# Two groups of value projections: the seven products in another order, and the last product's weight low parts made by a DMA

## Chip, core and metric

The kernel runs on one core of one Trainium2 chip. The metric is the device time of the whole program in microseconds, as the median of several executions.

## What is computed

Two transformer-like blocks over 512 tokens of 1,024 features. The change lies in the last mixer, hgrn2. Cut to what matters:

```python
def hgrn2_mixer(h, w_in, lb, norm_g, w_out):
    u = h @ w_in                              # (512, 1024) @ (1024, 8192)
    q, fz, i, gate = jnp.split(u, 4, axis=-1)
    ...                                       # i holds the values of 16 heads, 128 columns each
    o = hgrn2_chunk_scan(qc, kc, vc, bc)
    ...
    return (o * jax.nn.silu(gate)) @ w_out
```

The change touches only how `i`, the values (512 tokens by 2,048 columns), is projected.

## The kernel before

**Arithmetic.** Every fp32 operand of a matmul is kept as a high part, the fp32 value copied to the fp32r type that TensorE reads, and a low part, the value minus the high part. A product is three matmuls: high by high, high by low, low by high. ScalarE makes the high parts of the weights (an ACTIVATE that copies `RAW` to `WH`), VectorE the low parts (a TENSOR_TENSOR, `WL` = `RAW` - `WH`).

**The value stage.** The 2,048 value columns are done in two groups (`v` = 0 and 1 in `VG`). In each group the operands are cut in two by two blocks and seven products of block sums take the place of eight (Strassen's scheme in Winograd's form). The seven products carry the numbers 1 to 7: 1, 2 and 3 read a weight block as it came from memory (`b11`, `b21`, `b22`), 4 to 7 read a block into which VectorE has added or subtracted others in `block_sum`. Products 7, 6, 5 and 3 also need summed hidden states, made once and used by both groups: ScalarE makes their high parts (`ZR`, line 2716) and VectorE their low parts (`ER`, line 1784, four instructions for a product).

**Turns.** Each product comes in two halves (`u` = 0, 1), each with one 128 x 1024 weight tile and twelve 128x512 matmuls. This text calls a half a *turn*: `BLOCKS` lists 28 of them, turn 0 to turn 27, fourteen for a group, in the order of `BLOCK_ORDER`. Four buffers (`NS` = 4) hold weights for turns, so a turn uses the buffer of the turn four before it: ScalarE can write turn m's high part once TensorE has done with turn m - 4, and three turns lie between that moment and TensorE's need.

**Order of work.** Nothing is scheduled by a tool: each engine's program is written out by hand and runs in that order. On VectorE, `block_low(m)` makes the low part of turn m and behind some turns issues block sums for later ones, `hidden_low` makes a product's four `ER` parts, and `block_taken` adds a finished product's banks to the result (line 2026). On ScalarE, `block_high(m)` makes the high part (line 2866), `block_copied` copies a finished product out of two PSUM banks (line 2875) and so frees them, and `forget(0)`, `query(0)`, `scan_gate(0)` and `forget(1)` are gate work for the first two heads of the scan, put between. A product may start only when the banks it writes are free (`claim`). Banks 0 and 1 serve products 1, 6, 5 and 3 of the first group in turn.

**Loads.** SyncE issues all weight loads, 512 KB each, in one order (`load`, line 567). A load waits until the VectorE instruction that last needs its buffer is done. The tiles are kept in `RAW` and in parts of `TMP` and `Z` that are idle then. GpSimd has no program of its own.

TensorE's lines 1046, 1048 and 1049 are the three matmuls of a step in this stage. Lines 649 to 651 are those of the ordinary projections, and the first of them after the stage ends it.

Of the kernel before, what the change touches and what calls it, by code (L numbers as in the profile page):

```python
# [57 lines left out]
V1 = V0 + 8 * len(VG)  # L58
BLOCK_ORDER = (1, 7, 6, 2, 5, 4, 3)
BLOCKS = [(p, v, u) for v in range(len(VG)) for p in BLOCK_ORDER for u in range(2)]  # L60
# [83 lines left out]
def raw_list():  # L144
# [3 lines left out]
    for i, (name, n, _) in enumerate(UNITS):  # L148
        if NR <= i < NR + NX:
            slot = i  # L150
        elif name == "ada" and n >= 40:
            slot = NR + NX + n % 2
        elif name == "hgrn_in" and V0 <= n < V1:
            v, quarter, u = (n - V0) // 8, (n - V0) % 8 // 2, n % 2
            if v == 0 and quarter in (0, 3):
                slot = ring % NR
                ring += 1
                held[quarter, u] = slot
            else:
                slot = ((held[0, u], NR + NX + 4 + u, held[3, u], NR + NX + 2 + u) if v else  # L160
                        (None, NR + NX + 2 + u, NR + NX + 4 + u))[quarter]
        else:
            slot = ring % NR
            ring += 1
# [124 lines left out]
def build(nc, a):  # L289
    with ExitStack() as ctx:  # L290
# [133 lines left out]
        def block_source(m):  # L424
            p, v, u = BLOCKS[m]
            return raw(block_unit({1: 0, 6: 0, 3: 1, 7: 2, 5: 2, 2: 3, 4: 3}[p], v, u))

# [3 lines left out]
        def block_bank(p, v):  # L431
            return {7: 2, 4: 2, 2: 4}.get(p, 6 * v)

# [108 lines left out]
        hidden_done = Count(sem("s_hidden"))  # L542
        normed = Count(sem("s_normed"))
        wfree, zfree = {}, {}

# [8 lines left out]


        def sync_program(e):
            def load(i):
# [5 lines left out]
                elif RSLOT[i] >= NR + NX + 2 and RBEFORE[i] is None:  # L563
                    e.wait_ge(square.sem, square.of("pout", "x", 3))
                elif RBEFORE[i] is not None:
                    e.wait_ge(taken.sem, taken.of(RBEFORE[i]))
# [41 lines left out]
        def tensor_program(e):  # L608
# [422 lines left out]
            def block_product(p, v):  # L1031
# [268 lines left out]
        def vector_program(e):  # L1300
# [681 lines left out]
            def block_sum(p, v, u):  # L1982

                b11, b22, b12, b21 = (raw(block_unit(q, v, u)) for q in range(4))
                if p == 7:
                    e.wait_ge(*landed(block_unit(1, v, u)))
                    e.wait_ge(*landed(block_unit(2, v, u)))
                    to, x, y, op = b12, b22, b12, ALU.subtract
                elif p == 6:
# [13 lines left out]
            def block_low(m):  # L2003
                if m >= len(BLOCKS):
                    lo_to(p.unit + m - len(BLOCKS) + 1)
                    return
                i, v, u = BLOCKS[m]
                e.wait_ge(copied.sem, copied.of("block", m))
                hi, lo = block_place(m)
                e.tensor_tensor(lo, block_source(m), hi.bitcast(F32), ALU.subtract).then_inc(  # L2010
                    taken.sem, taken("block", m))
                for q in {5: (0, 2), 4: (3,), 3: (1,)}.get(i, ()):
# [98 lines left out]
            def first_sums():  # L2111
                hidden_sums("pout")
                block_low(0)
                hidden_low("pout", 7)
                block_low(1)
                hidden_low("pout", 6)
# [244 lines left out]
        def scalar_program(e):  # L2361
# [494 lines left out]
            def block_high(m):  # L2856
# [4 lines left out]
                if i in (1, 2, 3):  # L2861
                    e.wait_ge(*landed(block_unit({1: 0, 2: 3, 3: 1}[i], v, u)))
# [48 lines left out]
            def first_sums():  # L2911
                block_high(0)
                hidden_sum("pout", 7)
                block_high(1)
                for i in (6, 5, 3):
                    hidden_sum("pout", i)
# [180 lines left out]


        for program in (tensor_program, vector_program, scalar_program):
            program(Nothing())  # L3100
# [15 lines left out]
        def _(e):  # L3116
            vector_program(e)

        @block.scalar
# [120 lines left out]
```

## Time and profile before

| | before |
|---|---|
| median of 3 runs | 1406.69 us (1406.57 to 1407.81) |
| the profiled execution, its time | 1407.22 us |
| the profiled execution, its span | 1405.4 us |
| TensorE busy | 1390.7 us, 99% |
| VectorE busy | 983.0 us, 70% |
| ScalarE busy | 648.6 us, 46% |
| GpSimd busy | 0.2 us |
| mean busy share of the DMA engines by the window 0 to 100 us | 0.70 |
| the same, 900 to 1000 us | 0.30 |

The span runs from the first to the last instruction of the profiled execution, its time has 1.8 us more around it. An engine's busy time is the sum of its instructions with overlaps counted once. A high busy share of TensorE does not say how near it is to its peak, since matmuls overlap in its pipeline.

### The profile page before, as it was taken

The page shows a single profiled execution, that of the slowest core. Times are in us where ns is not written, and L with a number is a line of the kernel's source. Part 1 is how long each engine was busy: PE and PEld are TensorE (multiplying, and loading weights), DVE is VectorE, ACT ScalarE, POOL GpSimd, SP SyncE. Part 2 cuts the span into 40 slices and gives each one's busy share as a digit, 9 for nine tenths or more (in the row PEclk, how much of TensorE's full clock was granted, in tenths as well). Part 3 has the DMA queues.
Part 4 walks back from the last instruction along what each step waited for, and adds up shares of the span by engine and source line. Part 5 has one row for each costly group of instructions (what it writes and reads, how often), then busy time and mean ns, then how long its engine had stood idle before and what let it go on. Part 6 is the DMA issues. An engine that isn't in the chain of part 4 may idle for free.

```text
span 1405.4 us, 22088 instructions
## 1 busy us (share of the span) xinstructions
PE 1390.7 (99%) x8666; PEld 1190.9 (85%) x8666; DVE 983.0 (70%) x1922; ACT 648.6 (46%) x1268; POOL 0.2 (0%) x4
## 2 busy tenths in 40 slices
PE   8999999999999999999999999999999999999998
PEld 7888888999998888888888888978888888888886
DVE  7887777799953335755466535599798889888645
ACT  6423355567662324542332323575345555556441
POOL 0000000000000000000000000000000000000000
PEclk9999999999999999999999999999999999999999
DMA  9656441254333234032332233213322222221221
GB/s 353 226 186 243 150 162 68 91 172 146 117 107 105 90 103 152 31 105 90 103 107 75 91 116 124 91 47 121 104 91 75 76 76 77 75 76 61 76 75 60
DMA packets 43734, 158.00 MB, mean 112 GB/s; under 512 B 4848, under 2 KB 5232, under 8 KB 43632
## 3 DMA queue, kind: packets, MB, share of 16 engines
q1 hardware_dynamic: 43344, 156.39, 32.5%
q8 instruction: 69, 1.13, 0.3%
q14 instruction: 33, 0.27, 0.1%
q10 hardware_dynamic: 288, 0.21, 0.0%
HBM read 154.48 MB, written 2.10 MB: 111 GB/s over the span
## 4 chain that ended last, share of the span: by engine, by line
PE 95%; DVE 2%; issue 1%; ACT 1%; DMA 0%; SPq 0%; DVEq 0%; ACTq 0%
PE PS L649 26%; PE PS L651 25%; PE PS L650 25%; PE PS L990 3%; PE PS L992 3%; PE PS L991 3%; PE PS L1046 2%; PE PS L1048 2%; PE PS L1049 2%; PE PS L1147 1%; PE PS L1151 1%; PE PS L1139 1%; PE PS L645 1%; PE PS L1079 1%; PE PS L1160 0%
## 5 line engine op out<-in xcount | busy, mean ns | idle before, releaser
L649 PE MATMUL PS<-HH,WH 128*128 128x512 f32 (+1 forms) x880 | 337.3, 383 | 0.0
L651 PE MATMUL PS<-HH,WL 128*128 128x512 f32 (+1 forms) x880 | 332.8, 378 | 0.0
L650 PE MATMUL PS<-HL,WH 128*128 128x512 f32 (+1 forms) x880 | 332.5, 378 | 0.0
L2376 ACT ACTIVATE WH<-RAW 128x1024 fp32r<-128x1024 f32 x176 | 185.3, 1056 | 132.3 <-PE PS L651 86.7
L1371 DVE TENSOR_TENSOR WL<-RAW,WH 128x1024 fp32r<-128x1024 f32 x176 | 213.8, 1219 | 19.0 <-ACT WH L2376 18.6
L651 PEld LDWEIGHTS PS<-HH,WL 128*128 128x128 f32 x880 | 165.5, 188 | 31.3
L649 PEld LDWEIGHTS PS<-HH,WH 128*128 128x128 f32 x880 | 165.6, 188 | 30.7
L650 PEld LDWEIGHTS PS<-HL,WH 128*128 128x128 f32 x880 | 165.7, 188 | 29.3
L649 PE MATMUL PS<-WH,ZH 128*128 128x512 f32 x400 | 155.9, 390 | 0.0
L651 PE MATMUL PS<-WH,ZL 128*128 128x512 f32 x400 | 155.6, 389 | 0.0
L650 PE MATMUL PS<-WL,ZH 128*128 128x512 f32 x400 | 155.6, 389 | 0.0
L1422 DVE TENSOR_TENSOR ZL<-Z,ZH 128x512 fp32r<-128x512 f32 x52 | 35.6, 691 | 136.7 <-ACT ZH L2441 136.7
L2441 ACT ACTIVATE ZH<-Z 128x512 fp32r<-128x512 f32 x52 | 32.4, 632 | 149.2 <-PE PS L651 149.2
L651 PEld LDWEIGHTS PS<-WH,ZL 128*128 128x128 f32 x400 | 75.1, 188 | 15.7
L649 PEld LDWEIGHTS PS<-WH,ZH 128*128 128x128 f32 x400 | 75.1, 188 | 15.5 <-ACT Z L2751 0.2
L650 PEld LDWEIGHTS PS<-WL,ZH 128*128 128x128 f32 x400 | 75.1, 188 | 15.5
L990 PE MATMUL PS<-HH,WH 128*128 128x256 f32 x192 | 54.5, 284 | 1.4 <-DVE Z L1838 1.4
L992 PE MATMUL PS<-HH,WL 128*128 128x256 f32 x192 | 54.3, 283 | 0.0
L991 PE MATMUL PS<-ER,WH 128*128 128x256 f32 x192 | 54.3, 283 | 0.0
L2062 DVE RECIPROCAL DG<-W 128x96 f32<-128x96 f32 (+1 forms) x64 | 48.8, 814 | 0.0
L649 PE MATMUL PS<-WH,HH 128*128 128x512 f32 x96 | 39.2, 408 | 2.0 <-DVE RAW L1331 2.0
L2468 ACT ACTIVATE TMP<-X 128x1024 f32<-128x1024 f32 x18 | 19.0, 1056 | 47.9 <-DVE X L1486 29.9
(348 smaller groups left out, 2625.4 us busy)
## 6 DMA issues: line engine op xcount, KB each, us to landing
RAW<-in_w_fc SPq DMA_DIRECT2D x64, 512.0 KB, 3.3
RAW<-in_hgrn_in SPq DMA_DIRECT2D x56, 512.0 KB, 3.3
RAW<-in_pool_in SPq DMA_DIRECT2D x40, 512.0 KB, 3.3
RAW<-in_ada SPq DMA_DIRECT2D x36, 512.0 KB, 4.5
RAW<-in_w_in SPq DMA_DIRECT2D x26, 512.0 KB, 5.2
RAW<-in_pool_out SPq DMA_DIRECT2D x16, 512.0 KB, 3.3
RAW<-in_hgrn_out SPq DMA_DIRECT2D x16, 512.0 KB, 3.3
Z<-in_ada SPq DMA_DIRECT2D x12, 512.0 KB, 4.4
```

The source lines that it names most:

```text
L649: e.matmul(out, wh, xh, start=first, stop=False)
L650: e.matmul(out, wh, xl, start=False, stop=False)
L651: return e.matmul(out, wl, xh, start=False, stop=last)
L990: e.matmul(out, wh[:, k, :], xh[k], start=fresh and k == 0, stop=False, skip_group_check=True)
L991: e.matmul(out, wh[:, k, :], xl[k], start=False, stop=False, skip_group_check=True)
L992: mm = e.matmul(out, wl[:, k, :], xh[k], start=False, stop=k == 3, skip_group_check=True)
L1046: e.matmul(out, xh[k][:, cols], wh, start=k == 0 and p in (1, 2, 7), stop=False, skip_group_check=True)
L1371: e.tensor_tensor(lo, raw(i), hi.bitcast(F32), ALU.subtract).then_inc(taken.sem, taken(i))
L1422: e.tensor_tensor(lo, Z[:, k, :], hi.bitcast(F32), ALU.subtract).then_inc(zlo.sem, zlo(z))
L2062: e.reciprocal(i8[:, n, l], w8[:, n, l]).then_inc(own.sem, own("iw", h, i))
L2376: e.activation(place(s)[0], raw(i), ACT.Copy).then_inc(whi.sem, whi(s))
L2441: e.activation(z_place(z)[0], Z[:, k, :], ACT.Copy).then_inc(zhi.sem, zhi(z))
```

## The change

It does three things. (1) `BLOCK_ORDER` becomes 1, 2, 6, 7, 5, 4, 3, so that the two products that need no block sum (1 and 2) come first. The weight tiles are laid out in memory and loaded in the order `b11`, `b21`, `b22`, `b12`, the sums move to other turns, and products 2, 7 and 4 change banks. (2) The hidden parts of products 6 and 7 swap places, those of 5 and 3 move some turns later on VectorE, and two MEMSETs move from the stage's start to behind turn 9. (3) For product 3 (turns 12, 13, 26 and 27) VectorE no longer makes the low part. ScalarE writes the negated high part into `WL` by a second ACTIVATE behind the first, and GpSimd then issues a DMA that reads the weight tile from memory again and adds it to `WL`. TensorE waits for that DMA, and SyncE's loads into those tiles' buffers wait for ScalarE's second ACTIVATE.

```diff
-BLOCK_ORDER = (1, 7, 6, 2, 5, 4, 3)
+BLOCK_ORDER = (1, 2, 6, 7, 5, 4, 3)
...
         def block_bank(p, v):
-            return {7: 2, 4: 2, 2: 4}.get(p, 6 * v)
+            return {7: 4, 4: 4, 2: 2}.get(p, 6 * v)
...
+        ADDED = [m for m in range(len(BLOCKS)) if BLOCKS[m][0] == 3]
+        def block_added(m):
+            return s_added[block_slot(m)], 16 * sum(block_slot(x) == block_slot(m) for x in ADDED if x <= m)
...
+        last_blocks = {block_unit(2, v, u): m for m, (p, v, u) in enumerate(BLOCKS) if p == 3}
...
+                elif RBEFORE[i] in last_blocks:
+                    e.wait_ge(copied.sem, copied.of("minus", last_blocks[RBEFORE[i]]))
...
-                        e.wait_ge(taken.sem, taken.of("block", m))
+                        e.wait_ge(*(block_added(m) if m in ADDED else (taken.sem, taken.of("block", m))))
...
+                if m in ADDED:
+                    return
                 e.wait_ge(copied.sem, copied.of("block", m))
...
-                for to in {(1, 0): ((7, 0),), (1, 1): ((7, 1), (6, 0)), (7, 0): ((6, 1),), (7, 1): ((5, 0),),
-                           (6, 0): ((5, 1),), (2, 0): ((4, 0),), (2, 1): ((4, 1),)}.get((i, u), ()):
+                for to in {(1, 1): ((7, 0),), (2, 0): ((7, 1), (6, 0)), (2, 1): ((6, 1),), (6, 0): ((4, 0),),
+                           (6, 1): ((4, 1),), (7, 1): ((5, 0), (5, 1))}.get((i, u), ()):
...
             run(halved([[], []], first_sums))
             block_low(2)
-            hidden_low("pout", 5)
             p.unit += 8 * len(VG)
-            e.memset(IW[:, :], 1.0)
-            e.memset(W[:, :], 1.0).then_inc(own.sem, own("scan"))
-            e.wait_ge(own.sem, own.of("scan"))
             first_head = prepare(0)
             for n in range(len(BLOCKS) // 2):
                 block_low(2 * n + 3)
                 if n:
                     block_taken(*BLOCKS[2 * n - 2][0:2])
-                if n == 1:
-                    hidden_low("pout", 3)
+                if n in (1, 2):
+                    hidden_low("pout", 5 if n == 1 else 3)
                 if n == 3:
+                    e.memset(IW[:, :], 1.0)
+                    e.memset(W[:, :], 1.0).then_inc(own.sem, own("scan"))
+                    e.wait_ge(own.sem, own.of("scan"))
                     scan_gate(0)
...
                 e.activation(block_place(m)[0], block_source(m), ACT.Copy).then_inc(copied.sem, copied("block", m))
+                if m in ADDED:
+                    e.activation(block_place(m)[1], block_source(m), ACT.Copy, scale=-1.0).then_inc(
+                        copied.sem, copied("minus", m))
...
+        def pool_program(e):
+            for m in ADDED:
+                _, v, u = BLOCKS[m]
+                e.wait_ge(copied.sem, copied.of("minus", m))
+                e.dma_start(out=block_place(m)[1], in_=a["hgrn_in"][UNITS[block_unit(2, v, u)][1]],
+                            accum_op=ALU.add).then_inc(block_added(m)[0], 16)
```

In the rows below, `WL<-...,WH` (line 2010 before, 2024 now) is a low part, `ER<-E,ZR` a hidden low part, and any other TENSOR_TENSOR of 128x1024 a block sum.

VectorE at the start of the stage, from the low part of turn 1 on, before:

```order
L2010 TENSOR_TENSOR WL<-RAW,WH 128x1024
L2001 TENSOR_TENSOR TMP<-Z,TMP 128x1024
L2001 TENSOR_TENSOR RAW<-TMP,RAW 128x1024
L1784 TENSOR_TENSOR ER<-E,ZR 128x256 x4
L2010 TENSOR_TENSOR WL<-TMP,WH 128x1024
L2001 TENSOR_TENSOR RAW<-TMP,RAW 128x1024
L1784 TENSOR_TENSOR ER<-E,ZR 128x256 x4
L2122 MEMSET DG 128x512
L2123 MEMSET W 128x512
L2010 TENSOR_TENSOR WL<-TMP,WH 128x1024
L2001 TENSOR_TENSOR TMP<-Z,RAW 128x1024
L2010 TENSOR_TENSOR WL<-RAW,WH 128x1024
```

and now:

```order
L2024 TENSOR_TENSOR WL<-RAW,WH 128x1024
L2013 TENSOR_TENSOR TMP<-Z,TMP 128x1024
L1796 TENSOR_TENSOR ER<-E,ZR 128x256 x4
L2024 TENSOR_TENSOR WL<-RAW,WH 128x1024
L2013 TENSOR_TENSOR TMP<-Z,TMP 128x1024
L2013 TENSOR_TENSOR RAW<-TMP,RAW 128x1024
L2024 TENSOR_TENSOR WL<-RAW,WH 128x1024
L2013 TENSOR_TENSOR RAW<-TMP,RAW 128x1024
L2024 TENSOR_TENSOR WL<-RAW,WH 128x1024
L2013 TENSOR_TENSOR RAW<-RAW 128x1024
L2024 TENSOR_TENSOR WL<-RAW,WH 128x1024
L2013 TENSOR_TENSOR RAW<-RAW 128x1024
```

What stood between the low parts of turns 1 and 2 was two sums and an `ER` group. Now it is one sum and an `ER` group, and between the low parts of turns 2 and 3 the `ER` group and the two MEMSETs are gone.

VectorE further on, in front of the low parts of turns 8 and 9 (product 5), before:

```order
L2001 TENSOR_TENSOR RAW<-RAW 128x1024
L2010 TENSOR_TENSOR WL<-RAW,WH 128x1024
L2001 TENSOR_TENSOR RAW<-RAW 128x1024
L2010 TENSOR_TENSOR WL<-TMP,WH 128x1024 x2
L2032 TENSOR_TENSOR Z<-Z,PS6 128x512
L2010 TENSOR_TENSOR WL<-RAW,WH 128x1024 x2
L2026 TENSOR_TENSOR Z<-Z,PS34 128x4x128
L2026 TENSOR_TENSOR Z<-Z,PS5 128x4x128
```

and now, from the `ER` parts of product 5 on:

```order
L1796 TENSOR_TENSOR ER<-E,ZR 128x256 x4
L2024 TENSOR_TENSOR WL<-TMP,WH 128x1024 x2
L2013 TENSOR_TENSOR TMP<-Z,RAW 128x1024 x2
L2040 TENSOR_TENSOR Z<-Z,PS2 128x4x128
L2040 TENSOR_TENSOR Z<-Z,PS34 128x4x128
L1796 TENSOR_TENSOR ER<-E,ZR 128x256 x4
L2024 TENSOR_TENSOR WL<-TMP,WH 128x1024 x2
L2143 MEMSET DG 128x512
L2144 MEMSET W 128x512
```

What has left the start stands here: the two sums of product 5, the addition of product 2 (`Z<-Z,PS2` and `Z<-Z,PS34`) and the `ER` parts of product 3 now come between the low parts of turns 7 and 8.

ScalarE from the high part of turn 9 on, before:

```order
L2866 ACTIVATE WH<-TMP 128x1024
L2875 ACTIVATE Z<-PS0 128x4x128
L2875 ACTIVATE Z<-PS1 128x4x128
L2866 ACTIVATE WH<-RAW 128x1024 x2
L2866 ACTIVATE WH<-Z 128x1024 x2
L2866 ACTIVATE WH<-RAW 128x1024 x4
```

and now:

```order
L2879 ACTIVATE WH<-TMP 128x1024
L2891 ACTIVATE Z<-PS0 128x4x128
L2891 ACTIVATE Z<-PS1 128x4x128
L2879 ACTIVATE WH<-RAW 128x1024 x2
L2891 ACTIVATE Z<-PS34 128x4x128
L2891 ACTIVATE Z<-PS5 128x4x128
L2879 ACTIVATE WH<-Z 128x1024
L2881 ACTIVATE WL<-Z 128x1024
L2879 ACTIVATE WH<-Z 128x1024
L2881 ACTIVATE WL<-Z 128x1024
```

Each high part of product 3, now the first and second `WH<-Z`, is followed by a second ACTIVATE of the same size into `WL`. The copy of product 6 (`Z<-PS0`, `Z<-PS1`) stands behind the high part of turn 9 in both, but product 6 was turns 4 and 5 both times, while product 5, which needs its banks next, is at turns 8 and 9.

GpSimd has four DMAs into `WL` from `in_hgrn_in`, one for each turn of product 3, and nothing else of its own.

## Rows read from the trace of the kernel before

**Rows 1.** The page's head and its line on TensorE.

```profile
span 1405.4 us, 22088 instructions
PE 1390.7 (99%) x8666; PEld 1190.9 (85%) x8666; DVE 983.0 (70%) x1922; ACT 648.6 (46%) x1268; POOL 0.2 (0%) x4
```

**Rows 2.** Waits of TensorE: line, releaser, total us, times, longest.

```profile
PE PS L1046 <- DVE WL L2010: 1.8, 1, 1.8
PE PS L1046 <- issue: 0.6, 1, 0.6
```

**Rows 3.** TensorE timeline, product stage: start, us, line, tiles, idle before.

```profile
919.02 0.40 PE L1046 MATMUL PS<-WH,HH 128*128 128x512 f32 x1
919.25 0.40 PE L1048 MATMUL PS<-WL,HH 128*128 128x512 f32 x1
...
925.26 0.47 PE L1046 MATMUL PS<-WH,ZR 128*128 128x512 f32 x1 [0.62 <-issue]
...
930.03 0.50 PE L1046 MATMUL PS<-WH,ZR 128*128 128x512 f32 x1 [1.77 <-DVE WL L2010]
...
998.16 0.39 PE L649 MATMUL PS<-HH,WH 128*128 128x512 f32 x1
```

**Rows 4.** VectorE timeline of the same stage, same columns.

```profile
915.59 1.22 DVE L2010 TENSOR_TENSOR WL<-RAW,WH 128x1024 fp32r<-128x1024 f32 x1
916.72 1.22 DVE L2001 TENSOR_TENSOR TMP<-Z,TMP 128x1024 f32<-128x1024 f32 x1
917.86 1.43 DVE L1784 TENSOR_TENSOR ER<-E,ZR 128x256 fp32r<-128x256 f32 x4
919.20 1.22 DVE L2010 TENSOR_TENSOR WL<-RAW,WH 128x1024 fp32r<-128x1024 f32 x1
...
923.94 1.22 DVE L2010 TENSOR_TENSOR WL<-TMP,WH 128x1024 fp32r<-128x1024 f32 x1
...
928.75 1.22 DVE L2010 TENSOR_TENSOR WL<-TMP,WH 128x1024 fp32r<-128x1024 f32 x1
...
946.26 1.28 DVE L2026 TENSOR_TENSOR Z<-Z,PS 128x512 f32<-128x512 f32 x2
947.45 0.27 DVE L2046 COPY W<-Z 128x128 f32<-128x128 f32 x1
```

**Rows 5.** ScalarE timeline of the same stage, same columns.

```profile
922.55 0.58 ACT L2882 ACTIVATE Z<-PS 128x512 f32<-128x512 f32 x1
...
925.13 1.05 ACT L2866 ACTIVATE WH<-RAW 128x1024 fp32r<-128x1024 f32 x1
...
927.30 1.06 ACT L2875 ACTIVATE Z<-PS 128x512 f32<-128x512 f32 x2
928.25 0.60 ACT L2897 ACTIVATE Z<-PS 128x512 f32<-128x512 f32 x1
...
944.02 1.06 ACT L2866 ACTIVATE WH<-RAW 128x1024 fp32r<-128x1024 f32 x1 [1.66 <-PE PS L1049]
```

**Rows 6.** Loads of line 567 issued in 944.5:946, 949:950, 990:998.

```profile
L567 SPq DMA_DIRECT2D RAW<-in_hgrn_in x1: 327/327/327, 944.8 to 944.8; - x1
DMA to landing us min/median/max: 7.5/7.5/7.5
...
L567 SPq DMA_DIRECT2D Z<-in_hgrn_in x1: 327/327/327, 949.1 to 949.1; - x1
DMA to landing us min/median/max: 5.8/5.8/5.8
...
L567 SPq DMA_DIRECT2D RAW<-in_hgrn_in x2: 327/328/328, 992.6 to 995.3; - x2
DMA to landing us min/median/max: 3.1/3.2/3.4
```

**Rows 7.** Windows: us, busy by engine (count), PEclk, DMA share, GB/s.

```profile
950.00:952.00 2.00, 2.00 (x11) 1.65 (x10) 1.44 (x2) 0.52 (x1) 0.00 (x0) 1.00 1.02 418
...
984.00:988.00 4.00, 4.00 (x20) 3.30 (x19) 2.84 (x4) 1.52 (x2) 0.00 (x0) 1.00 0.59 229
```

More of the change, by code:

```diff
@@ L154, in raw_list @@
             v, quarter, u = (n - V0) // 8, (n - V0) % 8 // 2, n % 2
-            if v == 0 and quarter in (0, 3):
+            if v == 0 and quarter in (0, 1):
                 slot = ring % NR
@@ L159, in raw_list @@
             else:
-                slot = ((held[0, u], NR + NX + 4 + u, held[3, u], NR + NX + 2 + u) if v else
-                        (None, NR + NX + 2 + u, NR + NX + 4 + u))[quarter]
+                slot = ((held[0, u], NR + NX + 4 + u, held[1, u], NR + NX + 2 + u) if v else
+                        (None, None, NR + NX + 2 + u, NR + NX + 4 + u))[quarter]
         else:
@@ L425, in block_source @@
             p, v, u = BLOCKS[m]
-            return raw(block_unit({1: 0, 6: 0, 3: 1, 7: 2, 5: 2, 2: 3, 4: 3}[p], v, u))
+            return raw(block_unit({1: 0, 6: 0, 2: 1, 4: 1, 3: 2, 7: 3, 5: 3}[p], v, u))
+        ADDED = [m for m in range(len(BLOCKS)) if BLOCKS[m][0] == 3]
+        def block_added(m):
+            return s_added[block_slot(m)], 16 * sum(block_slot(x) == block_slot(m) for x in ADDED if x <= m)
         def block_place(m):
@@ L543, in build @@
         normed = Count(sem("s_normed"))
+        s_added = [sem(f"s_added{i}") for i in range(NS)]
         wfree, zfree = {}, {}
@@ L1982, in block_sum @@
             def block_sum(p, v, u):
-                b11, b22, b12, b21 = (raw(block_unit(q, v, u)) for q in range(4))
+                b11, b21, b22, b12 = (raw(block_unit(q, v, u)) for q in range(4))
                 if p == 7:
-                    e.wait_ge(*landed(block_unit(1, v, u)))
                     e.wait_ge(*landed(block_unit(2, v, u)))
+                    e.wait_ge(*landed(block_unit(3, v, u)))
                     to, x, y, op = b12, b22, b12, ALU.subtract
@@ L2011, in block_low @@
                     taken.sem, taken("block", m))
-                for q in {5: (0, 2), 4: (3,), 3: (1,)}.get(i, ()):
+                for q in {5: (0, 3), 4: (1,)}.get(i, ()):
                     taken.at[block_unit(q, v, u),] = taken.n
-                for to in {(1, 0): ((7, 0),), (1, 1): ((7, 1), (6, 0)), (7, 0): ((6, 1),), (7, 1): ((5, 0),),
-                           (6, 0): ((5, 1),), (2, 0): ((4, 0),), (2, 1): ((4, 1),)}.get((i, u), ()):
+                for to in {(1, 1): ((7, 0),), (2, 0): ((7, 1), (6, 0)), (2, 1): ((6, 1),), (6, 0): ((4, 0),),
+                           (6, 1): ((4, 1),), (7, 1): ((5, 0), (5, 1))}.get((i, u), ()):
                     block_sum(to[0], v, to[1])
@@ L2113, in first_sums @@
                 block_low(0)
+                hidden_low("pout", 6)
+                block_low(1)
                 hidden_low("pout", 7)
-                block_low(1)
-                hidden_low("pout", 6)
             run(halved([[], []], first_sums))
             block_low(2)
-            hidden_low("pout", 5)
             p.unit += 8 * len(VG)
-            e.memset(IW[:, :], 1.0)
-            e.memset(W[:, :], 1.0).then_inc(own.sem, own("scan"))
-            e.wait_ge(own.sem, own.of("scan"))
             first_head = prepare(0)
@@ L2861, in block_high @@
                 if i in (1, 2, 3):
-                    e.wait_ge(*landed(block_unit({1: 0, 2: 3, 3: 1}[i], v, u)))
+                    e.wait_ge(*landed(block_unit({1: 0, 2: 1, 3: 2}[i], v, u)))
                 else:
@@ L2912, in first_sums @@
                 block_high(0)
-                hidden_sum("pout", 7)
+                hidden_sum("pout", 6)
                 block_high(1)
-                for i in (6, 5, 3):
+                for i in (7, 5, 3):
                     hidden_sum("pout", i)
@@ L3117, in _ @@
             vector_program(e)
+        @block.gpsimd
+        def _(e):
+            pool_program(e)
         @block.scalar
@@ L3226 @@
             groups(np.concatenate([hin[:, c:c + 128] for c in (2048, 0, 6144, 2176)], 1)),
-            groups(hin[:, 4096:6144])[[0, 1, 6, 7, 4, 5, 2, 3, 8, 9, 14, 15, 12, 13, 10, 11]],
+            groups(hin[:, 4096:6144])[[0, 1, 2, 3, 6, 7, 4, 5, 8, 9, 10, 11, 14, 15, 12, 13]],
             qfg.reshape(48, 128, 1024)[4:]]),
```

## Prediction

> **What bounds the kernel now.** The page comes first: TensorE is busy 1390.7 of 1405.4 us [rows 1], so nothing that shortens VectorE, ScalarE or a transfer pays unless TensorE waits for it, and all its idle time is 14.7 us. The list of its waits comes next. In the stage of the value products it has two, 1.8 us on a low part of VectorE and 0.6 us that the list puts down to issue [rows 2]. The timeline of TensorE sizes them. Matmuls there start 0.23 us apart. From 930.03 to 998.16 it does 25 turns in 68.1 us, 2.72 us each, without a stall. The 28 turns should take 76.2 us and take 79.1 (919.02 to 998.16), so 2.98 us are lost [rows 3]. Turn 2 starts at 925.26 instead of 924.46 and turn 3 at 930.03 instead of 927.98, that is 0.80 and 2.05 us, and 0.13 us are restarts. The timeline of VectorE says why: the low part of turn 2 runs from 923.94 to 925.16, that of turn 3 from 928.75 to 929.97, each ending just before TensorE starts [rows 3, 4]. VectorE has worked without a gap since 915.59 and is simply behind. So the order has at most 2.98 us to give back, 0.21% of the whole.
>
> **The change, VectorE's new order.** From one start to the next, a low part or a block sum takes 1.14 us, a group of four `ER` parts 1.34 us, and the two additions of a finished product 1.19 us; a low part is done 1.22 us after it starts [rows 4]. I lay the new order out from the same 915.59, TensorE from 919.02 at 2.72 us a turn.
> Turn 2: three 1.14 us instructions and two `ER` groups stand before its low part, which starts at 921.7 and ends at 922.9, against 924.5 when it is needed.
> Turn 3: two sums and a low part more, done at 926.3 against 927.2.
> Turns 4 to 7 come out at 928.6, 930.8, 934.5 and 935.6 against 929.9, 932.6, 935.3 and 938.1, all in time, turn 6 by 0.8 us only.
> Turn 8: before its low part stand 8 low parts, 8 sums, four `ER` groups and one pair of additions, 16 x 1.135 + 4 x 1.34 + 1.19 = 24.7 us. It starts at 940.3 and ends at 941.5, and TensorE wants it at 940.8. So part of the old debt comes back there, 0.8 us.
> ScalarE makes it a little worse. Turn 8 is product 5, which needs the banks of product 6. Their copy stands on ScalarE behind the high part of turn 8 (which waits for a sum that VectorE ends at 936.7), behind `forget(1)` and behind the high part of turn 9. `forget` takes 2.58 us (922.55 to 925.13), a high part 0.97 from start to start, and one half of the copy 0.6 [rows 5]: 936.7 + 0.97 + 2.58 + 0.97 = 941.2, the first bank is free at 941.8, and TensorE starts at 941.9, 1.1 us late. I take this, as the later of the two.
> From turn 9 on VectorE is ahead again, each low part ending 1 us or more before its turn. Banks elsewhere are free in time, the tightest for turn 4: its banks come free at 929.0 and 929.5, against 929.9 and 930.6.
> So the order removes 2.98 us and adds 1.1 and a restart of 0.1, a gain of 1.8 us.
>
> **The low part of product 3.** VectorE loses four instructions, 4.5 us, worth nothing by themselves, since it is behind only up to turn 8. The two MEMSETs are hidden behind its lead from turn 9 on. ScalarE gains four ACTIVATEs, 3.9 us. It waits 1.66 us for TensorE before the high part of one turn after another [rows 5], which covers them; without that cover each would put off a high part by 0.97 us. Behind the second ACTIVATE of turn 12 stands the high part of turn 13, behind that of turn 13 the one of turn 14, and both have over 5 us to spare. SyncE's loads into the buffers that product 3 releases go out when that ACTIVATE is done, where before they waited for VectorE, about a microsecond apart, and nothing needs them for 7 us.
> What decides is the DMA. Turn 12's buffer is free at 944.9, but ScalarE still has the high part of turn 11 and the copy of product 7 before it: high part of turn 12 from 945.1, second ACTIVATE from 946.1 to 947.1. TensorE, 1.1 us late, wants turn 12 at 919.0 + 1.1 + 12 x 2.72 = 952.8. That leaves 5.6 us from issue to landing. Turn 13 has 5.9 us (949.6 to 955.5), turns 26 and 27 about 5.9 each.
> No DMA from GpSimd and no accumulating one stands in the trace. The nearest rows are the plain loads of the same 512 KB. Alone they land in 3.1 to 3.4 us. In the crowd of the second group's loads they take 7.5 (issued at 944.8) and 5.8 (issued at 949.1) [rows 6], with the DMA engines full at 418 GB/s [rows 7], which is 1.25 us for 512 KB. The first pair of new DMAs falls into just that crowd, seven loads having been issued by 947.2. Behind all of them it would land in some 7 us, but it comes on a queue of its own. Sharing the engines half and half it needs 2 x 1.25 and the 1.9 us that a lone load takes beyond its bytes, 4.4 us. Between 4.4 and 7.5 I take 6.0 for both pairs: turn 12 is late by 0.4, turn 26 by 0.1. The bounds are 3.1 us (no stall) and 7.5 + 1.25 = 8.8 us (last in the crowd, bytes moved twice), where turns 12 and 26 are 3.2 and 2.9 late and the gain of 1.8 becomes a loss of 4.3.
> The Trainium skill has a price for a plain DMA issued from GpSimd (DMA: Bandwidth & Descriptors, Anatomy of one DMA — SWDGE): about 2.0 us and the bytes at 436 GB/s, by which this one would be an estimated 3.2 us and the gain the full 1.8. No run here shows it yet.
>
> **Sum.** -1.8 + 0.5 = -1.3 us: from the profiled execution's 1407.2 us to 1405.9, and from the median of the runs, 0.5 lower at 1406.69, to 1405.4. What a measurement of this kernel can tell from no change is 0.2%, 2.8 us, so this counts as no change.
>
> **The rivals.**
> *Bytes twice* (0.22). An addition in memory must read the old `WL` as well as the weights. If the engines spend twice the time on it, the first DMA shares the crowd half and half and needs 4 x 1.25 + 1.9 = 6.9 us, landing at 954.1 instead of 952.8. The second queues behind it and lands 5.0 us later, at 959.1, where TensorE wants it at 956.8. That is 1.3 + 2.3 = 3.6 us. The second pair meets one load: 3 x 1.25 + 1.9 = 5.7, in time. Sum +1.8, to 1408.5. For it speaks that DMA share is at 1.02 there, against it only that most of the crowd may have passed. The Trainium skill speaks for it (Collectives: The Full Stack, The bandwidth ceiling): an adding DMA costs no ALU time but reads two sources through one ring, and ran at about half the rate of a copy.
> *The DMA's way is slow* (0.18), the one that ends on the other side. GpSimd runs 0.2 us of work in the whole program [rows 1], so nothing shows what it takes to issue, above all the first time. From issue to landing L, the stalls are (L - 5.6) + (L - 5.9). The gain is used up at L = 6.7 us, and the loss passes 0.2% at L = 8.1. At 10 us the sum is -1.8 + 8.5 = +6.7, to 1413.4.
> *The reordering gives nothing* (0.07). VectorE's new order is tight at turns 3, 4 and 6 by 0.8 to 1.3 us, and a slip of that size, on a bank or a sum, puts the debt back at another turn: 1406.7, or with the DMA's 0.5, 1407.2.
> *All is in time* (0.03). If turn 8 too comes in time and the DMAs land within 5 us, the whole 2.98 is gained: 1403.7, the one case beyond 0.2% downward.
>
> **How the numbers follow.** The forecast, 1404.9 (no stall) to 1406.7 (L up to 6.7), has 0.50. With bytes twice and the empty reordering that is 0.79, and the range that holds 8 in 10 must take in their spread and the bound of L = 8.8 us: 1404.2 to 1411.0. Slower by over 0.2% is the slow way, 0.18, and a quarter of bytes twice, 0.05; faster by over 0.2% is 0.03; the rest, 0.74, is within it.
>
> **What would show it.** In the profile after: TensorE without idle time before turns 2 and 3, and one stall of 0.5 to 1.5 us at turn 8 (about 941), put down to ScalarE's copy or the low part on VectorE. Low parts 24 instead of 28, ScalarE 3.9 us busier, and GpSimd's DMAs issued near 947, 950, 985 and 988. The landing time of those DMAs is the step to look at: 4.4 to 6.7 us right, over 8 wrong. If turn 13 waits longer than turn 12, it is bytes twice; if turns 12 and 26 wait alike and 13 and 27 not at all, it is latency. The prediction is wrong if stalls stand at turns 2 to 6, or if what TensorE wins here it loses to new waits after the stage.

## The result: 8.8 us slower

The changed kernel takes 1416.01 us (median of 4 runs, 1414.73 to 1416.12), the kernel before, run beside it, 1407.25 (4 runs). The ratio is 1.0058 (95%: 1.0046 to 1.007), slower by more than the 0.2% that can be told, and above the forecast of 1405.4 and its range. The profiled execution took 1416.12 us with a span of 1414.3, 8.9 more than before [rows 1].

The page of the changed kernel, its head, its engines and its two queues that move data:

```profile
span 1414.3 us, 22092 instructions
PE 1395.2 (99%) x8666; PEld 1194.0 (84%) x8666; DVE 978.2 (69%) x1918; ACT 652.1 (46%) x1272; POOL 3.8 (0%) x8
...
q1 hardware_dynamic: 43344, 156.39, 32.4%
q0 software_dynamic: 576, 2.10, 0.8%
```

VectorE has four instructions less, ScalarE four more and is 3.5 us busier, as planned. TensorE is *busier* by 4.5 us at the same number of matmuls, so about half of the 8.9 us shows as no wait at all. Its waits in this stage (line, releaser, total us, times, longest; line 1058 is line 1046 of before):

```profile
PE PS L1058 <- issue: 3.8, 1, 3.8
PE PS L1058 <- DMA WL<-in_hgrn_in: 2.2, 2, 1.9
...
PE PS L1058 <- ACT Z L2891: 1.0, 1, 1.0
```

The two waits of before [rows 2] are gone, three other rows with four waits stand in their place. The timeline of TensorE places them (the stage, the same columns as [rows 3]):

```profile
918.44 0.40 PE L1058 MATMUL PS<-WH,HH 128*128 128x512 f32 x1
...
941.38 0.47 PE L1058 MATMUL PS<-WH,ZR 128*128 128x512 f32 x1 [0.99 <-ACT Z L2891]
...
956.35 0.76 PE L1058 MATMUL PS<-WH,ZR 128*128 128x512 f32 x1 [3.84 <-issue]
956.91 0.63 PE L1060 MATMUL PS<-WL,ZR 128*128 128x512 f32 x1
957.34 0.63 PE L1061 MATMUL PS<-WH,ER 128*128 128x512 f32 x1
957.76 0.63 PE L1058 MATMUL PS<-WH,ZR 128*128 128x512 f32 x1
...
997.76 0.50 PE L1058 MATMUL PS<-WH,ZR 128*128 128x512 f32 x1 [0.26 <-DMA WL<-in_hgrn_in]
...
1002.69 0.50 PE L1058 MATMUL PS<-WH,ZR 128*128 128x512 f32 x1 [1.90 <-DMA WL<-in_hgrn_in]
```

The first rows are turns 0, 8 and 12, the last two turns 26 and 27. Against 2.72 us from one start to the next, turn 8 comes 1.15 us late, turn 12 4.00, turn 26 0.42 and turn 27 2.21. The list puts the wait of turn 12 down to "issue"; the timeline of GpSimd says what it is. Its four DMAs (line 3119):

```profile
946.80 1.01 POOL L3119 DMA_DIRECT2D WL<-in_hgrn_in  x1 [946.36 <-ACT WL L2881]
949.49 0.86 POOL L3119 DMA_DIRECT2D WL<-in_hgrn_in  x1 [1.68 <-ACT WL L2881]
991.74 0.86 POOL L3119 DMA_DIRECT2D WL<-in_hgrn_in  x1 [41.39 <-ACT WL L2881]
994.52 0.89 POOL L3119 DMA_DIRECT2D WL<-in_hgrn_in  x1 [1.93 <-ACT WL L2881]
```

The first two go out on time (forecast 947.1 and 949.6), the last two 6.7 and 6.5 us behind the forecast of 985 and 988, since by then the whole stage is 6.9 us late. They land 9.5, 10.6, 6.0 and 8.1 us after their issue. For the first:

```profile
L3119 POOL DMA_DIRECT2D WL<-in_hgrn_in x1: 1008/1008/1008, 946.8 to 946.8; - x1
...
DMA to landing us min/median/max: 9.5/9.5/9.5
```

946.8 + 9.5 = 956.3, and TensorE starts turn 12 at 956.35.

Where these 9.5 us go, the DMA view of two windows tells (queue: packets, MB, share of 16 engines' time; queue 0 is GpSimd's, queue 1 SyncE's, and one of GpSimd's DMAs has 144 packets). From 946.8 to 951.1:

```profile
q1 hardware_dynamic: 450, 1.64, 102.2%
```

and from 951.1 to 956.3:

```profile
q0 software_dynamic: 172, 0.64, 62.8%
q1 hardware_dynamic: 216, 0.78, 41.7%
```

For 4.3 us after its issue not one packet of the DMA starts. All that start are SyncE's, and most of those belong to loads issued ahead of it. Its own packets and its landing take the other 5.1 us.

Between the matmuls at 956.91, 957.34 and 957.76 lie 0.43 us where it was 0.23: nearly the whole turn 12 runs at half speed. Windows of the same kernel (us, busy time of TensorE, its weight loads, VectorE, ScalarE and GpSimd with counts, granted clock, DMA share, GB/s):

```profile
946.00:948.00 2.00, 2.00 (x10) 1.68 (x9) 1.93 (x6) 1.33 (x2) 1.01 (x1) 1.00 1.04 414
952.00:956.30 4.30, 0.51 (x3) 0.09 (x1) 2.09 (x3) 1.06 (x1) 0.00 (x0) 0.91 1.05 271
956.50:961.50 5.00, 5.00 (x12) 3.94 (x13) 3.08 (x4) 0.00 (x0) 0.00 (x0) 0.50 0.81 242
1002.70:1006.60 3.90, 3.90 (x10) 3.10 (x11) 1.96 (x4) 0.15 (x1) 0.00 (x0) 0.58 0.73 267
```

The granted clock is 1.00 before the stall (2.4 GHz), 0.50 in the 5 us behind it (1.2 GHz) and 0.58 behind the stall of turn 27. "PE busy" counts this as work; only the clock column or the distance of the starts shows it. And while TensorE waits for the DMA, the DMA engines are full (share 1.05) but move 271 GB/s, where before they moved 418 at the same share [rows 7].

**The account.** The stage runs from 918.44 to 1007.14, where the first matmul of line 661 starts:

```profile
1006.63 0.44 PE L1060 MATMUL PS<-WL,ZR 128*128 128x512 f32 x1
1006.91 0.39 PE L1061 MATMUL PS<-WH,ER 128*128 128x512 f32 x1
1007.14 0.40 PE L661 MATMUL PS<-HH,WH 128*128 128x512 f32 x1
```

In it 12.5 us are lost against 28 x 2.72, before it was 2.98. Turn 8: 1.15 and a restart of 0.09. Waits for the DMAs: 4.00 + 0.42 + 2.21 at turns 12, 26 and 27, and 1.0 at turn 13, whose weights land at 949.5 + 10.6 = 960.1 while turn 12 at full speed would have ended at 959.1: 7.7 us. Half clock: turn 12 is longer by 2.53, turn 13 by 0.38, turn 27 by 1.73, 4.6 in all, less the 1.0 that turn 12 hides, 3.6 us. The new order's gain is 2.98 - 1.27 = 1.7. So -1.7 + 7.7 + 3.6 = +9.6 us, which is what the stage lost more (12.54 - 2.98). The span grew by 8.9 only, because in this execution the stage began 0.58 us earlier than before; behind the stage the two executions agree within 0.1 us.

### The profile page after: what moved, and what is told of

Same layout as the page of the kernel before. It is cut to its first block, busy times and chain, and to the rows that moved or that the text cites. A ratio compares the mean times of both kernels' runs of the same rounds, so it can differ in the third digit from the quotient of the medians.

```text
span 1414.3 us, 22092 instructions
## 1 busy us (share of the span) xinstructions
PE 1395.2 (99%) x8666; PEld 1194.0 (84%) x8666; DVE 978.2 (69%) x1918; ACT 652.1 (46%) x1272; POOL 3.8 (0%) x8
## 4 chain that ended last, share of the span: by engine, by line
PE 93%; DVE 3%; issue 1%; DMA 1%; ACT 1%; SPq 0%; POOL 0%; DVEq 0%; ACTq 0%; POOLq 0%
PE PS L661 25%; PE PS L663 25%; PE PS L662 25%; PE PS L1002 3%; PE PS L1004 3%; PE PS L1003 3%; PE PS L1058 1%; PE PS L1061 1%; PE PS L1060 1%; PE PS L1159 1%; PE PS L1163 1%; PE PS L1151 1%; PE PS L657 1%; DMA WL<-in_hgrn_in 1%; PE PS L1091 1%
```

## The experiments

Line numbers are those of each kernel; where an edit shifts nothing they are the changed kernel's. "Before" is always the kernel before in the same rounds.

### The order alone: order_only

```diff
-        ADDED = [m for m in range(len(BLOCKS)) if BLOCKS[m][0] == 3]
+        ADDED = [m for m in range(len(BLOCKS)) if BLOCKS[m][0] == 3 and False]
```

VectorE makes the low parts of product 3 again, at the places of the new order, and SyncE's loads into those buffers wait for it again. (second_group and odd_only treat the turns without a DMA in the same way.)

> The changed kernel's order, with VectorE making the low parts of product 3 as before and no DMA from GpSimd. Theory A (the order gains, the DMA loses): TensorE keeps the one stall of 1.15 us at turn 8, the stage loses 1.3 us instead of 2.98, and the time is 1.7 us under the kernel before, ratio about 0.999. Rival (the order itself costs something, for example at turns 13 to 20): the time is above the kernel before.

1405.28 us (11 runs) against 1406.7; ratio 0.9985 (0.9976 to 0.9994): 1.4 us won of the 1.8 forecast. TensorE's waits in the stage are one row:

```profile
PE PS L1058 <- ACT Z L2891: 1.0, 1, 1.0
```

In the stage 1.29 us are lost instead of 2.98. The half of the change that moves instructions does what the prediction said, and the loss is all in the DMAs.

### The DMAs alone: dma_only

The kernel before with its own `BLOCK_ORDER`, and from the change only the second ACTIVATE, the DMAs of GpSimd and the waits for them.

```diff
+                if m in ADDED:
+                    e.activation(block_place(m)[1], block_source(m), ACT.Copy, scale=-1.0).then_inc(
+                        copied.sem, copied("minus", m))
...
+        def pool_program(e):
+            for m in ADDED:
+                e.wait_ge(copied.sem, copied.of("minus", m))
...
+                            accum_op=ALU.add).then_inc(block_added(m)[0], 16)
```

> The kernel before in its own order, with the second ACTIVATE and the adding DMA for product 3. If the DMA's loss does not depend on the order: the stalls at turns 2 and 3 (2.8 us) stay, the waits at turns 12, 13, 26 and 27 and the half clock come on top with 8 to 11 us, time 8 to 11 us over the kernel before. Rival (the new order of loads is what makes the crowd): the first pair lands in under 8 us and the time is under 6 us over.

1412.09 us (4 runs) against 1406.91; ratio 1.0041 (1.0026 to 1.0056). Landings 9.4, 10.5, 5.5 and 5.5 us; turn 12 waits 3.87 and is then 1.69 longer, turn 27 waits 0.04. The time over the kernel before, 5.2 us, is below the 8 to 11 expected: the first pair is as slow as with the new order, the second pair is not. In this order SyncE's next loads go out at 997.4 and 1000.1, behind the second pair, in the changed kernel at 991.5, 994.2, 997.2 and 999.9, among it.

### Only the second group's: second_group

```diff
-        ADDED = [m for m in range(len(BLOCKS)) if BLOCKS[m][0] == 3]
+        ADDED = [m for m in range(len(BLOCKS)) if BLOCKS[m][0] == 3 and BLOCKS[m][1] == 1]
```

> The changed kernel with the DMA for the second group only (turns 26 and 27); turns 12 and 13 get their low parts from VectorE. If each pair of DMAs pays by itself: the second pair's stalls of 0.42 and 2.21 us and 1.2 us of half clock stay, 3.8 us, and against the order's gain of 1.7 the time is about 2 us over the kernel before, 6.9 us under the changed kernel. Rival (the first DMA of the program pays for its being first, the others do not): turn 26, now the first, waits some 3 us more, and the time is 4 to 6 us over the kernel before.

1408.9 us (10 runs) against 1406.7; ratio 1.0012 (1.0003 to 1.0021). Without a first pair the second lands in 7.0 and 9.1 us instead of 6.0 and 8.1. Being GpSimd's first DMA costs at most this microsecond and is not what makes the pair at 946.8 slow. The profile is of the longest of the ten executions, 1410.96 us, 2.1 above their median. In it turns 26 and 27 wait 1.46 and 2.11 us, and the clock falls again:

```profile
997.40:1001.20 3.80, 3.80 (x11) 3.02 (x12) 2.03 (x4) 0.28 (x1) 0.00 (x0) 0.61 0.58 215
```

### Without the addition: plain_pool

The same DMAs without `accum_op`. The low part of product 3 is then the whole weight, so the kernel computes something else; its work and its waits are the same.

```diff
-                e.dma_start(out=block_place(m)[1], in_=a["hgrn_in"][UNITS[block_unit(2, v, u)][1]],
-                            accum_op=ALU.add).then_inc(block_added(m)[0], 16)
+                e.dma_start(out=block_place(m)[1], in_=a["hgrn_in"][UNITS[block_unit(2, v, u)][1]]).then_inc(
+                    block_added(m)[0], 16)
```

> The four DMAs from GpSimd without the addition, so that the low part of product 3 is the whole weight and its result is another; bytes, queue and times of issue are as in the changed kernel. Theory twice (the addition makes the DMA engines work twice on each byte): landings fall from 9.5, 10.6, 6.0 and 8.1 us to about 6.5, 6.5, 3.8 and 4.5, turn 12 waits under 1.5 us, no half clock, time within 1 us of the kernel before or below. Rival path (what GpSimd does to issue is slow): landings stay within 1 us of the changed kernel's, and so does the time, 8 to 9 us over the kernel before.

1408.33 us (10 runs) against 1406.7; ratio 1.0006 (0.9997 to 1.0015). Landings 7.7, 7.5, 4.3 and 4.4 us. Turns 26 and 27 no longer wait; turn 12 waits 2.19, and then runs at half speed for 1.69 more (clock 0.61). So without the addition 7 of the 8.8 us are gone, though turn 12 was expected to wait under 1.5 us and to keep its clock. The DMA view of 935 to 1010 us says what an addition costs the engines (queue: packets, MB, share of 16 engines' time). Changed kernel:

```profile
q1 hardware_dynamic: 2304, 8.39, 32.2%
q0 software_dynamic: 576, 2.10, 14.4%
```

And plain_pool:

```profile
q1 hardware_dynamic: 2304, 8.39, 31.0%
q0 software_dynamic: 576, 2.10, 7.6%
```

The four DMAs take 14.4% of 75 us with the addition, 2.7 us each, and 7.6%, 1.4 us each, without: 1.9 times as much. The rate of a plain one equals that of SyncE's loads (31.0% for 16 of them, 1.45 us each). GpSimd also issues faster, 0.66 and 0.53 us instead of 1.01 and 0.86.

### The clock held up: filler and filler_fit

Ahead of each of the four turns TensorE runs matmuls on operands at hand into bank 2, whose results nothing uses. They keep it busy while it would wait.

```diff
+                    if m in ADDED and k % 2 == 0:
+                        for _ in range({12: 18, 13: 5, 26: 2, 27: 8}[m]):
+                            e.matmul(PS[2][:, :], HH[:, 0, 0:128], HH[:, 1, :], start=True, stop=True)
```

In filler the four numbers were 24, 8, 8 and 16.

> The changed kernel with matmuls on a free PSUM bank put before TensorE's waits for the DMAs: 24 before turn 12, 8 before turns 13 and 26, 16 before turn 27, of 128x512, results unused. Theory clock (the long stall brings the granted clock to 0.5, which costs 4.1 us more): the fill of 5.4 us keeps the clock at 1.0, turns 12 and 13 take 2.7 us each, and though TensorE is held longer by the fill itself (up to 1.5 us at turn 12 and 1.5 us in the others), the time is 1 to 3 us under the changed kernel. Rival (the half clock has another cause than the idle time, such as the DMAs): the granted clock still falls to 0.5, and the time is over the changed kernel's.

> As filler, with the fill cut to the waits: 18, 5, 2 and 8 matmuls. Theory clock: the granted clock stays at 1.0 through turns 12 and 13 and after turn 27, each turn takes 2.7 us, and the stage loses what the landings cost alone, 8 to 9 us, instead of 12.0: time 3 to 4 us under the changed kernel. Rival (the fill only moves the loss): the time is that of the changed kernel within 1 us.

filler: 1417.87 us (4 runs) against 1406.7; ratio 1.0074 (1.006 to 1.0088). The fill was too long: the turns came 5.44, 1.81, 1.82 and 3.72 us late, and turns 12, 13 and 27 started 0.7, 1.3 and 2.2 us after their DMAs had landed. So this tells nothing of the clock's price. filler_fit: 1414.17 us (4 runs) against 1407.42; ratio 1.0048 (1.0034 to 1.0062). Here the turns come 4.17, 1.79, 0.53 and 1.99 late, 8.5 us, and each starts within 0.05 us of its DMA's landing (956.60, 961.10, 997.12 and 1001.83), so the fill itself holds up none. The landings are 9.7, 11.5, 6.1 and 8.0 us in this execution, and the delays by 0.8 us more than the 7.7 above. The clock is at 1.00 throughout:

```profile
952.00:956.00 4.00, 4.00 (x19) 3.32 (x18) 2.22 (x3) 1.06 (x1) 0.00 (x0) 1.00 1.06 277
956.00:962.00 6.00, 5.68 (x25) 4.09 (x24) 4.20 (x5) 1.06 (x1) 0.00 (x0) 1.00 0.78 228
```

The stage loses 10.05 us instead of 12.5, 2.5 less, and 3.3 less if the later landings are counted in, near the account's 3.6. So the fallen clock follows from TensorE's idling, not from the DMAs themselves. Expected were a stage loss of 8 to 9 us and 3 to 4 us of time won. (The 12.0 us of this expectation, and the 4.1 of half clock in the one before, take the stage's end 0.5 us too early.) The medians differ by 1.8 us, and the two ratios' intervals overlap: the stage shows the gain, the time alone would not.

### A DMA away from the crowd: probe

The kernel before, and after the stage eight DMAs of GpSimd one behind another into tiles that nothing reads by then, plain and adding in turn, to fp32 and to fp32r.

```diff
+                if i % 2:
+                    e.dma_start(out=to, in_=a["hgrn_in"][i], accum_op=ALU.add).then_inc(s_probe, 16)
+                else:
+                    e.dma_start(out=to, in_=a["hgrn_in"][i]).then_inc(s_probe, 16)
+                e.wait_ge(s_probe, 16 * (i + 1))
```

> The kernel before with eight DMAs of 512 KB from GpSimd after the value stage, one after another, each waited for by GpSimd alone, into a tile that nothing reads then: plain and adding in turn, into fp32 and into fp32r. The output is not touched. Theory twice: alone a plain one lands in 3.5 to 4.5 us and an adding one 1.0 to 1.6 us later than that, whatever the type. Rival (the path is slow the first time): the first of the eight takes 2 us or more over the fifth. Rival (the change of type costs): those into fp32r take over 1 us more.

One execution (1406.73 us). Plain ones (line 3108) and adding ones (line 3106):

```profile
L3108 POOL DMA_DIRECT2D E<-in_hgrn_in x2: 550/620/689, 1016.8 to 1038.7; - x2
...
DMA to landing us min/median/max: 3.6/4.5/4.7
...
L3106 POOL DMA_DIRECT2D E<-in_hgrn_in x2: 877/878/879, 1020.7 to 1043.6; - x2
...
DMA to landing us min/median/max: 5.4/5.5/7.1
```

In order of time: plain 3.6, adding 7.1, plain 4.6, adding 5.5, plain 4.5, adding 5.4, plain 4.7, adding 5.5. The first is the fastest of all, and the type makes no difference. A load of SyncE alone takes 3.1 to 3.4 [rows 6]. But these eight were not alone: SyncE's ordinary loads went on, and at least one was in flight during part of each. The first plain one met the least of them. An adding DMA with no other in flight is the first of dma_only's second pair. It lands in 5.5 us, 1.6 of them before its first packet. So the addition adds 0.9 us with a load beside both, and up to 1.9 with next to none. The forecast of 6.0 would be nearly right for a DMA alone.

### One of each pair: odd_only

A rival by then: each adding DMA is held up by the one before it on GpSimd's queue.

```diff
+        ADDED = [m for m in range(len(BLOCKS)) if BLOCKS[m][0] == 3 and BLOCKS[m][2] == 1]
```

> The changed kernel with the DMA only for the second half of product 3 in each group (turns 13 and 27), so that no adding DMA has another before it. Theory twice and queue: turn 27 lands in 6 to 7 us instead of 8.1 and waits under 1.2 us, turn 13, still in the crowd, lands in 8 to 9.5 us and waits 2 to 3.5 us; time 1 to 4 us over the kernel before. Rival (the landing time is latency of its own and not the queue): landings stay at 10.6 and 8.1 us, turns 13 and 27 wait 4.7 and 2.2 us, time 5 us over or more.

1414.15 us (4 runs) against 1406.91; ratio 1.0048 (1.0034 to 1.0062). The DMAs of turns 13 and 27, now with none before them, land in 10.4 and 7.9 us, as in the changed kernel (10.6, 8.1). So the one before is not what makes them late, and the rival has fallen. The packets give it one point: in the changed kernel queue 0 has started 170 packets by 956.2, when the first DMA, of 144, is about to land, so the second, issued at 949.5, had started 26 packets by then at most. Without the first, its packets start at 954.1, 4.6 us after the issue, and still run until 959.6. Turn 13 waits 4.85 us, since turn 12 is now in time and at full speed and hides nothing of it; turn 27 waits 2.32. The windows ahead of turn 13, in its wait and behind, and behind turn 27's wait:

```profile
953.00:955.00 2.00, 2.00 (x11) 1.55 (x9) 1.25 (x2) 0.72 (x1) 0.00 (x0) 1.00 1.06 301
955.00:960.00 5.00, 0.32 (x3) 0.03 (x1) 5.00 (x6) 1.06 (x1) 0.00 (x0) 1.00 0.64 159
960.00:964.40 4.40, 4.40 (x12) 3.51 (x13) 2.17 (x3) 0.00 (x0) 0.00 (x0) 0.61 0.00 0
...
1002.10:1006.00 3.90, 3.90 (x39) 3.01 (x43) 1.71 (x4) 1.45 (x3) 0.00 (x0) 1.00 0.55 187
```

The last one is the window behind the wait of turn 27: there the clock stayed up.

### SyncE's loads held back: held_loads

The loads into the buffers that product 3 releases wait until the adding DMA of that turn has landed.

```diff
-                    e.wait_ge(copied.sem, copied.of("minus", last_blocks[RBEFORE[i]]))
+                    e.wait_ge(*block_added(last_blocks[RBEFORE[i]]))
```

> The changed kernel, but SyncE's loads into the buffers of product 3 wait until the adding DMA has landed instead of going out with it, and all loads behind them with them. Theory crowd: with fewer loads beside it turn 12's DMA lands in 7.5 to 9 us instead of 9.5, turn 13's in 5.5 to 8 instead of 10.6, those of turns 26 and 27 in 5.4 to 6 instead of 6.0 and 8.1; turn 27 no longer waits; time 3 to 6 us under the changed kernel, if the later loads are still in time. Rival (landing does not depend on the loads beside it): landings within 0.5 us of the changed kernel's, time the same or higher for the later loads.

1410.27 us (10 runs) against 1407.42; ratio 1.0022 (1.0012 to 1.0031). Landings 8.6, 8.4, 5.3 and 5.4 us. With no load going out between 946.9 and 956.1 (in the changed kernel three did, at 946.6, 949.2 and 949.6), the first pair lands 0.9 and 2.2 us sooner, the second, with no load beside it until 994.4, 0.7 and 2.7 sooner, as fast as alone. So one transfer's crowd is what the others issue *after* it as well as before. The packets divide the two. The first DMA's first packet starts 4.6 us after its issue, as late as ever, and from there it lands in 4.0 us, against 5.1 in the changed kernel and 3.9 for the one alone in dma_only. The three loads now held back had cost the 1.2 us; the wait for the first packet belongs to those ahead of them. Turn 12 still waits 3.11 us, and the second pair's turns not at all. And in this execution the clock stayed up:

```profile
953.00:956.10 3.10, 0.21 (x1) 0.00 (x0) 1.79 (x2) 1.06 (x1) 0.00 (x0) 1.00 1.08 218
956.10:959.00 2.90, 2.84 (x13) 2.36 (x13) 0.00 (x0) 0.00 (x0) 0.00 (x0) 1.00 0.99 280
```

This profile is of the shortest of the ten executions, 1408.9 us. The others took 0.5 to 3.0 us more at a mean granted clock of 0.996 to 0.998 (0.998 in this one), so the clock may well have fallen behind turn 12 in some of them.

### The stall at turn 8 removed: order_fixed and order_fixed2

Both are order_only, VectorE making all low parts. ScalarE copies product 6 before `forget(1)`, and one pair of additions and one `ER` group are moved behind the low part of turn 8.

order_fixed puts them behind low part 9, together with the two MEMSETs of the gate work, and the high part of turn 9 behind `forget(1)`:

```diff
-                if n:
+                if n and n != 2:
...
+                    block_taken(2, 0)
+                    hidden_low("pout", 3)
```

order_fixed2 puts them between low parts 8 and 9, and leaves the high part of turn 9 ahead of `forget(1)`:

```diff
+                if n == 2:
+                    block_taken(2, 0)
+                    hidden_low("pout", 3)
...
+                if n == 3:
+                    forget(1)
...
-                    forget(1)
+                    block_copied(6, 0)
```

> The new order without the DMAs, and the stall of turn 8 taken away: ScalarE copies product 6 before forget(1), VectorE adds product 2 and makes the hidden low parts of product 3 behind the low part of turn 9. If the 1.15 us at turn 8 are the only loss left: the stage loses 0.1 us, the time is 1.2 us under the order alone and 2.6 to 2.9 us under the kernel before, ratio 0.998. Rival (the debt only moves to another turn): a stall of 0.5 us or more at turns 9 to 13 and a time within 0.5 us of the order alone.

> As order_fixed, but the work is moved elsewhere: VectorE adds product 2 and makes the hidden parts of product 3 between the low parts of turns 8 and 9, where order_fixed left it 3.3 us of idle time, and ScalarE makes the high part of turn 9 before forget(1). If the first try failed only by where it put the work: no stall over 0.1 us in the stage, time 2.6 to 2.9 us under the kernel before, ratio 0.998. Rival (the debt of VectorE is too large to hide in these turns): a stall at turn 9, 10 or 11 again, time not under that of the order alone.

order_fixed: 1408.35 us (11 runs) against 1406.91; ratio 1.0009 (1.0 to 1.0017). A difference this small would say little, but it is 3.1 us above order_only and the stage shows why. Turn 8 is in time, but a new wait stands at turn 10, the row of TensorE's waits and then VectorE's timeline:

```profile
PE PS L1058 <- DVE WL L2024: 2.5, 1, 2.5
```

```profile
938.15 1.23 DVE L2024 TENSOR_TENSOR WL<-TMP,WH 128x1024 fp32r<-128x1024 f32 x1
942.65 1.22 DVE L2024 TENSOR_TENSOR WL<-TMP,WH 128x1024 fp32r<-128x1024 f32 x1 [3.27 <-ACT WH L2881]
943.79 1.28 DVE L2040 TENSOR_TENSOR Z<-Z,PS 128x512 f32<-128x512 f32 x2
944.99 1.43 DVE L1796 TENSOR_TENSOR ER<-E,ZR 128x256 fp32r<-128x256 f32 x4
946.47 0.48 DVE L2145 MEMSET DG<- 128x512 f32 x1
```

VectorE stands idle 3.27 us for the high part of turn 9, which is now late behind `forget(1)`, with the moved work queued behind low part 9, and then does that work ahead of low part 10. Turn 10 waits 2.75 us and runs 1.73 longer at a clock of 0.61, with no DMA of GpSimd in the kernel.

order_fixed2: **1403.9 us** (10 runs, 1403.66 to 1404.57) against 1407.42; ratio 0.9975 (0.9966 to 0.9985). The moved work now stands where VectorE was idle, and the high part of turn 9 starts at 939.0 instead of 941.6. Both were changed at once, so how much each is worth is not shown. TensorE has no wait in the stage, from 919.32 to 995.51 it loses 0.03 us. This beats the kernel before by 3.5 us and the changed one by 12.1. The stage can give only 2.98 of the 3.5, and the two profiled spans differ by 2.6; the kernel before had a median 0.2 to 0.7 us higher in these rounds than in the others here.

## Why the prediction was wrong

**Right: the order.** Turns 2 to 7 came in time and turn 8 was late by 1.15 us (forecast 1.1), by ScalarE's copy of product 6 and not by the low part, which VectorE ended at 941.0, 0.4 us before TensorE started. In the stage the order won 1.7 us (forecast 1.8), in the medians of order_only 1.4. The rival that the reordering gives nothing has fallen, and order_fixed2 shows that the full 2.98 us were to be had.

**Right: the budgets.** The first pair of DMAs was issued within 0.3 us of the forecast and had 5.6 us to the start of turn 12, as written. ScalarE's four extra ACTIVATEs and VectorE's four fewer were worth nothing, and there was no new loss behind the stage.

**Wrong: "Between 4.4 and 7.5 I take 6.0 for both pairs".** Measured were 9.5, 10.6, 6.0 and 8.1 us, three of the four above 7.5 and two beyond the upper bound of 8.8, so the term of 0.5 us for stalls came to 7.7. The runs take 9.5 apart as follows. Alone an adding DMA lands in 5.5 us, 1.6 to its first packet and 3.9 from there (the first of dma_only's second pair). In the crowd it was 4.3 to the first packet and 5.1 from there. The first excess, 2.7 us, goes with the loads issued ahead of it: it is there for a plain DMA too (3.9 us to the first packet in plain_pool) and stays when later loads are held back (4.6 in held_loads). The second, 1.2 us, goes when they are held back (4.0 from the first packet on). The second DMA's excess, 5.1 us, was not taken apart in this way.

So the step that failed first is "Sharing the engines half and half it needs 2 x 1.25". A queue of its own did not let the DMA share from its issue on: for 4.3 us it had no packet started. And once it moved, the addition made its packets take 1.9 times the engines' time.

I had also costed the crowd as if it were the seven loads issued by 947.2. It does not end there: SyncE issues further ones at 949.2 and 949.6, and they too slow the adding DMAs and are slowed themselves. The four loads issued between 946.2 and 949.6 took 8.3, 11.7, 11.0 and 12.8 us, in order_only 6.5, 6.5, 5.7 and 7.7. That the change itself sends SyncE's loads out "about a microsecond apart, and nothing needs them for 7 us" was true, and I did not ask what they do to the DMA beside them. The same holds for the second pair, which I took to be nearly alone.

**The rival "bytes twice"** was right in substance, an adding DMA takes 1.9 times the engines' time, and wrong in what makes the second late: taking the first away does not bring it forward (odd_only), the competitor is SyncE's queue, and the price is higher than the +3.6 worked out. Neither of the prediction's two signs came: turn 13 did not wait longer than turn 12, nor did turns 12 and 26 wait alike, and turn 27 waited more than turn 26. The rule of the Trainium skill (Collectives: The Full Stack, The bandwidth ceiling) that an addition on the DMA engines reads two sources, and in a collective ran at about half the rate of a copy, agrees with 14.4% against 7.6%. The Trainium skill's price for a plain DMA from GpSimd (DMA: Bandwidth & Descriptors, Anatomy of one DMA — SWDGE), by which I had an estimated 3.2 us, is low here: 3.6 us measured with next to no load beside it, 4.3 to 4.7 with one or two. **The rival of the slow way** gave the formula (L - 5.6) + (L - 5.9), with one stall for each pair; with the measured 9.5 and 8.1 it gives 3.9 + 2.2 = 6.1, and 1.0 for turn 13 and 0.4 for turn 26 are missing from it.

**Not in the sum at all: the clock.** The stalls brought the granted clock to half for the turn behind, 3.6 us net by the account and 2.5 to 3.3 by filler_fit. The trace of before had a hint that I read as "restarts", 0.13 us at short waits [rows 3]; its longest wait in this stage, turn 3's 2.05 us, was followed by no such fall.

## What to carry to other kernels

An accumulating DMA takes work off an engine, but here it cost nearly twice a copy's time on the DMA engines and landed 5.5 us after its issue when alone and in 6.0 to 11.5 us among loads. So in a kernel like this it needs either some twelve microseconds of slack or a stretch in which no other queue issues. The loads already under way count, since they delay its first packet, and so do those that go out until it lands. A wait of TensorE of 2 to 5 us can cost another 1.7 to 2.5 us in clock behind it, which the busy column hides: look at the granted clock in a window behind each wait. Where an engine is merely behind for a few turns, ordering its work anew is cheaper than moving the work elsewhere, but moved work must land where the engine would be idle: two placements of nearly the same work came out at 1408.35 and 1403.9 us.

## What the runs showed of the hardware

- The clock's fall does not follow from the length of the wait alone. Behind waits of 4.0 (changed), 3.87 (dma_only), 4.85 (odd_only), 2.19 (plain_pool), 2.75 (order_fixed) and 2.1 to 2.2 us (turn 27 of second_group and changed) the granted clock was 0.50 to 0.61 over the next 4 to 5 us. Behind one of 3.11 (held_loads) and one of 2.32 (turn 27 of odd_only) it stayed at 1.00, and behind the 2.05 of turn 3 in the kernel before the next turns took 2.72 us as ever [rows 3]. Each of these is one profiled execution. What decides between them stays open.
- The first packet of a DMA of GpSimd issued into the first group's crowd started 3.9 to 4.6 us after its issue (changed, plain_pool, dma_only, held_loads, odd_only), with the engines idle after 1.6 (the first of dma_only's second pair). A queue of its own gave it no turn in between.
- A full DMA share says nothing about the rate: a share of 1.04 stood beside 414 GB/s with plain loads alone and one of 1.05 beside 271 with adding ones among them.
- GpSimd spends 0.86 to 1.01 us on issuing an adding DMA of 512 KB, 0.53 to 0.69 on a plain one.
